# Modulation steps ahead of the scan's item, each fold with its own PSUM pair, in a one-core diffusion step

## The chip, the cores and the metric

The kernel runs on one core of a Trainium2 chip. The metric is the device time of one execution in microseconds (us). Before the change it is 2715.37 us, the median of three runs (2713.58 to 2716.63).

## The reference

One layer of a diffusion backbone works on 128 prompt tokens and 512 sample tokens, all in fp32, width 2048. Cut to what matters here:

```python
mod = silu(c) @ w_ada[l] + b_ada[l]              # 6 sections of 2048, for c and for c_ctx
sh1, sc1, g1, sh2, sc2, g2 = split(mod, 6)
h = x * (1 + sc1) + sh1
z = h @ w_in                                     # q, k, v, g, gate inputs, pooled part
log_a = log_sigmoid(a @ w_a2 + b_a) / 16         # per head, per direction
o, s = gla_chunked(q, k, v, log_a, s0)           # chunked scan, forward and backward, 4 heads
m = concat(rms_norm(o) * gain * silu(g), pool(p)) @ w_out
x = layer_norm(ALPHA * x + g1 * m)
h = x * (1 + sc2) + sh2
x = layer_norm(ALPHA * x + g2 * (silu(gate) * up) @ w_down)
```

Two of the six modulation sections, sh1 and sc1, are needed at once. The other four (sh2, sc2, g1, g2) are computed beside the projection `z = h @ w_in`, in stretches of TensorE that this document is about.

## The kernel before, in words

Every engine has its own program, written out by hand, and all of them walk one list, `SCHEDULE`. The list follows 33 units of `w_in`, each 128 output columns. A unit is four quarters (`main`) of 24 matmuls of 320 columns, since fp32 products are made of three matmuls of rounded parts (L2031 to L2033). ScalarE copies a unit's result out of PSUM (`evac`) and rounds the weights of a later unit (L977); VectorE forms their rest (L1377).

Between two quarters TensorE may leave the projection for an excursion. An excursion holds one item of the scan of a head `h` and a direction `d`, and until the modulation is done two ada steps, here called the pair of steps. The items are

- `gate`: the gate's matmul (L2072, from L2112); then VectorE takes a minimum (L1529), ScalarE the absolute value (L1129), exponential and logarithm, and VectorE the cumulative sum,
- `vT`: five transposes of v (L2103), which ScalarE copies out (L1122),
- `score`: five transposes (L2120) and then twenty records of small matmuls (L2126), with the copy L1144 and the masking L1562 behind them,
- `outer` and `outer9` (L2072, from L2144), nine outer products, which VectorE adds up to the states,
- `mix`: the output of the scan (L2161, L2166), copied or added out by VectorE (L1616 to L1619); later `norm` turns the result (L2174), after VectorE has scaled it (L1638).

An ada step multiplies 512 rows of `w_ada` (1 MB, loaded by SyncE, L689, into a ring of two slots) into four groups of 32 rows of PSUM bank 3 (L2011). After four steps ScalarE copies the bank to `high` (`adarow`, L1172). In the next excursion with a slot this row is folded: either two records of one matmul and a copy by ScalarE (`adasum`, L2191 and L1180, after which SyncE stores the row, L723), or four short matmuls and an addition by VectorE (`adacol`, L2198 and L1412). `SLOT` marks where the pair and a fold stand; `INNER` is a pair without a fold, between `outer` and `outer9`.

PSUM banks 4 and 5 are pair A, 6 and 7 are pair B. `add_pairs` gives every item its pairs in the order of the list: gate A, vT B, score B for the transposes and A for the products, outer and mix A and B, `adasum` B, `adacol` A. Before an item writes to a pair, TensorE waits in `take` until the pair's previous content has been drained.

Of the kernel before, what the change touches and what calls it, by code (L numbers as in the profile page):

```python
# [177 lines left out]
N_ADA = 16  # L178
ADA_STEPS = 4 * N_ADA
X_LOAD, X_NORM = 116, 119  # L180
SLOT, INNER = ("slot", 0, 0), ("slot", 1, 0)


def make_schedule():


    steps = []
    for n, (kind, h, j, _) in enumerate(PLAN):
        gap = [[], [], [], []]
        steps.append([n, gap])  # L190

    def put(n, quarter, *items):
        n, quarter = n + quarter // 4, quarter % 4
        steps[n][1][quarter].extend(items)

    where = {(k, h, j): n for n, (k, h, j, _) in enumerate(PLAN)}
    for h in range(HEADS):

        after_k = 4 * (where["k", h, 0] + 1)
        for at, item in ((1, ("wa", h, 0)), (2, ("state", h, 0)), (2, SLOT), (4, ("gate", h, 0)), (4, SLOT),  # L200
                         (6, ("vT", h, 0)), (6, SLOT), (6, ("cum", h, 0)), (8, ("score", h, 0)), (8, SLOT),
                         (10, ("vT", h, 1)), (10, SLOT), (12, ("outer", h, 0)), (12, INNER), (12, ("outer9", h, 0)),
                         (14, ("mix", h, 0)), (14, SLOT), (14, ("final", h, 0)),
                         (16, ("state", h, 1)), (16, ("gate", h, 1)), (16, SLOT), (18, ("cum", h, 1)),
                         (20, ("score", h, 1)), (20, SLOT),
                         (22, ("outer", h, 1)), (22, INNER), (22, ("outer9", h, 1)),
                         (24, ("mix", h, 1)), (24, SLOT), (24, ("final", h, 1)), (25, ("square", h, 0)),
                         (26, ("rms", h, 0)), (27, ("norm", h, 0)), (29, ("o_store", h, 0))):
            put(0, after_k + at, item)
    for j in range(8):  # L210
        put(where["p", j // 2, j % 2], 4, ("pool", j // 2, j % 2))
    for t in range(TT):
        if t == 0:
            put(0, X_LOAD, ("x_load", 0, 0))
        put(0, X_NORM + 2 * t, ("x_norm", t, 0))
    for g in range(4):
        put(where["p", g, 1], 7, ("poolmm", g, 0))
    flat = []
    for n, gap in steps:
        for quarter in range(4):  # L220
            flat.append(("main", n, quarter))
            if quarter == 3:
                flat.append(("evac", n, 0))
            flat.extend(gap[quarter])
    return with_modulation(flat)


def with_modulation(flat):


    out, done, behind = [], 0, []
    for item in flat:
        if item not in (SLOT, INNER):
            out.append(item)
            continue
        last = None
        if done < ADA_STEPS:
            out += [("ada", done // 4, done % 4), ("ada", done // 4, done % 4 + 1)]
            done += 2
            last = done // 4 - 1 if done % 4 == 0 else None  # L240
        if item == SLOT:
            for a in behind:
                if ADA[a // 4][1] == "col":
                    out.append(("adacol", a, 0))
                else:
                    out += [("adasum", a, 0), ("row_store", a, 0)]
            behind = []
        if last is not None:
            out.append(("adarow", last, 0))
            behind.append(last)  # L250
    assert done == ADA_STEPS and not behind
    return out


def add_pairs(flat, fills):


    used = [0, 0]
    need = {"gate": "A", "score": "AB", "outer": "AB", "outer9": "A", "mix": "AB", "norm": "AB",
            "vT": "B", "poolmm": "AB", "adasum": "B", "adacol": "A"}  # L260
    out = []
    for kind, a, b in flat:
        uses = []
        for c in need.get(kind, ""):
            x = "AB".index(c)
            uses.append((x, used[x]))
            used[x] += 1
        out.append((kind, a, b, uses))
    fills.extend(used)
    return out  # L270


FILLS = []
SCHEDULE = add_pairs(make_schedule(), FILLS)
USES = {(kind, a, b): uses for kind, a, b, uses in SCHEDULE}

# [45 lines left out]
def backbone(nc, x_all, state_gla, w_ada, w_in_b, wa2, w_pool_l, w_out, w_gu_b, w_down, consts,  # L322
# [333 lines left out]
    def _(sp):  # L656
# [144 lines left out]
        for i in range(2, N_OUT):  # L801
# [3 lines left out]
            if i == 4:  # L805
                for x in range(2):
                    sp.wait_ge(spilled[x], 16 * n_out[x])
                    sp.wait_ge(drained[x], FILLS[x])
                sp.wait_ge(row_out, 16 * 8)
# [1183 lines left out]
    def _(pe):  # L1993
# [210 lines left out]
        for x in range(2):  # L2204
            pe.wait_ge(drained[x], FILLS[x])

# [239 lines left out]
```

## Time and profile before

| | |
|---|---|
| profiled execution | 2721.88 us |
| its span | 2720.1 us |
| busy: TensorE matmul | 2643.3 us (97%) |
| busy: VectorE | 1424.9 us (52%) |
| busy: ScalarE | 898.4 us (33%) |
| busy: GpSimd | 652.8 us (24%) |
| mean granted TensorE clock | 0.991 of full speed |

TensorE is busy nearly throughout. Busy time of matmuls is modelled, since they are pipelined, so what a stretch of TensorE costs is better read from the start of one group of matmuls to the start of the next. The excursions with pairs of steps lie between about 140 and 545 us of the span; the scan of the last head, the pooling and the output projection follow.

### The profile page before, as it was taken

The page shows a single profiled execution, that of the slowest core. Times are in us where ns is not written, and L with a number is a line of the kernel's source. Part 1 is how long each engine was busy: PE and PEld are TensorE (multiplying, and loading weights), DVE is VectorE, ACT ScalarE, POOL GpSimd, SP SyncE. Part 2 cuts the span into 40 slices and gives each one's busy share as a digit, 9 for nine tenths or more (in the row PEclk, how much of TensorE's full clock was granted, in tenths as well). Part 3 has the DMA queues.
Part 4 walks back from the last instruction along what each step waited for, and adds up shares of the span by engine and source line. Part 5 has one row for each costly group of instructions (what it writes and reads, how often), then busy time and mean ns, then how long its engine had stood idle before and what let it go on. Part 6 is the DMA issues. An engine that isn't in the chain of part 4 may idle for free.

```text
span 2720.1 us, 37395 instructions
## 1 busy us (share of the span) xinstructions
PE 2643.3 (97%) x16040; PEld 2354.7 (87%) x16040; DVE 1424.9 (52%) x1680; ACT 898.4 (33%) x940; POOL 652.8 (24%) x218
## 2 busy tenths in 40 slices
PE   5999999998999999999999999999999999999997
PEld 3787877797988879999999999999999888888875
DVE  5323232346576457655555545555566354444578
ACT  4333333332311154333333333333333333333343
POOL 0000000000000001344443444344434333333440
PEclk9999999999999989999999999999999999999998
DMA  9775757422463142332233323332334645464566
GB/s 378 281 277 209 272 207 255 153 90 91 176 218 118 64 159 80 108 108 88 93 108 108 96 86 106 108 103 84 101 108 158 239 174 213 174 213 166 208 231 233
DMA packets 179384, 438.11 MB, mean 161 GB/s; under 512 B 9980, under 2 KB 25732, under 8 KB 173076
## 3 DMA queue, kind: packets, MB, share of 16 engines
q1 hardware_dynamic: 176916, 430.48, 45.4%
q10 hardware_dynamic: 2304, 5.24, 0.5%
q8 instruction: 127, 2.08, 0.3%
q14 instruction: 37, 0.30, 0.0%
HBM read 401.83 MB, written 33.85 MB: 160 GB/s over the span
## 4 chain that ended last, share of the span: by engine, by line
PE 62%; DVE 11%; DMA 10%; POOL 10%; issue 4%; ACT 3%; SPq 0%; POOLq 0%; ACTq 0%; DVEq 0%
PE ps L2355 6%; PE ps L2356 6%; PE ps L2357 6%; DMA raw_w<-w_gu_b 5%; PE ps L2278 5%; PE ps L2280 5%; PE ps L2279 5%; PE ps L2031 5%; PE ps L2033 5%; PE ps L2032 5%; POOL raw_w L945 3%; PE ps L2011 3%; DVE w_lo L1666 3%; POOL low L942 2%; POOL raw_w L948 2%
## 5 line engine op out<-in xcount | busy, mean ns | idle before, releaser
L1666 DVE TENSOR_TENSOR w_lo<-raw_w,w_hi 128x1024 fp32r<-128x1024 f32 x264 | 336.6, 1276 | 297.6 <-ACT w_hi L1210 294.7
L1210 ACT ACTIVATE w_hi<-raw_w 128x1024 fp32r<-128x1024 f32 x264 | 270.1, 1054 | 601.0 <-POOL raw_w L951 368.9
L2278 PE MATMUL ps<-x_hi,w_hi 128*128 128x320 f32 x1408 | 435.7, 309 | 1.0 <-DVE w_lo L1666 0.7
L2279 PE MATMUL ps<-x_lo,w_hi 128*128 128x320 f32 x1408 | 435.1, 309 | 0.0
L2280 PE MATMUL ps<-x_hi,w_lo 128*128 128x320 f32 x1408 | 435.1, 309 | 0.0
L942 POOL TENSOR_TENSOR low<-raw_w 128x1024 f32<-128x1024 f32 x41 | 103.7, 2528 | 1098.8 <-DMA raw_w<-w_gu_b 1058.7
L1801 DVE TENSOR_TENSOR x_lo<-low,x_hi 128x2560 fp32r<-128x2560 f32 (+2 forms) x55 | 221.3, 4027 | 262.6 <-ACT x_hi L1303 262.6
L2355 PE MATMUL ps<-w_hi,x_hi 128*128 128x512 f32 x880 | 343.8, 391 | 7.7 <-DVE w_lo L1932 2.8
L2356 PE MATMUL ps<-w_lo,x_hi 128*128 128x512 f32 x880 | 343.1, 390 | 0.0
L2357 PE MATMUL ps<-w_hi,x_lo 128*128 128x512 f32 x880 | 342.9, 390 | 0.0
L2278 PE MATMUL ps<-low_r,w_hi 128*128 128x320 f32 x1072 | 333.0, 311 | 1.5 <-DVE w_lo L1666 1.5
L2279 PE MATMUL ps<-low_r,w_hi 128*128 128x320 f32 x1072 | 332.2, 310 | 0.0
L2280 PE MATMUL ps<-low_r,w_lo 128*128 128x320 f32 x1072 | 332.1, 310 | 0.0
L2031 PE MATMUL ps<-x_hi,w_hi 128*128 128x320 f32 x1024 | 322.9, 315 | 1.8 <-DVE x_lo L1434 1.8
L2033 PE MATMUL ps<-x_hi,w_lo 128*128 128x320 f32 x1024 | 316.6, 309 | 0.0
L2032 PE MATMUL ps<-x_lo,w_hi 128*128 128x320 f32 x1024 | 316.5, 309 | 0.0
L956 POOL TENSOR_TENSOR w_lo<-raw_w,w_hi 128x2048 fp32r<-128x2048 f32 x45 | 212.5, 4723 | 352.5 <-ACT w_hi L1312 352.5
L2278 PEld LDWEIGHTS ps<-x_hi,w_hi 128*128 128x128 f32 x1408 | 264.4, 188 | 1.8 <-DVE w_lo L1666 1.3
L2279 PEld LDWEIGHTS ps<-x_lo,w_hi 128*128 128x128 f32 x1408 | 264.4, 188 | 0.0
L2280 PEld LDWEIGHTS ps<-x_hi,w_lo 128*128 128x128 f32 x1408 | 264.3, 188 | 0.0
L1377 DVE TENSOR_TENSOR w_lo<-raw_w,w_hi 128x2048 fp32r<-128x2048 f32 x48 | 110.0, 2291 | 262.8 <-ACT w_hi L977 262.7
L1312 ACT ACTIVATE w_hi<-raw_w 128x2048 fp32r<-128x2048 f32 x55 | 105.4, 1916 | 380.6 <-PE ps L2357 364.5
(238 smaller groups left out, 4362.9 us busy)
## 6 DMA issues: line engine op xcount, KB each, us to landing
raw_w<-w_gu_b SPq DMA_DIRECT2D x180, 512.0 KB, 5.6
low<-w_ada SPq DMA_DIRECT2D x68, 1024.0 KB, 6.9
raw_w<-w_down SPq DMA_DIRECT2D x55, 1024.0 KB, 5.2
low<-hidden_scratch SPq DMA_DIRECT2D x33, 1280.0 KB, 6.0
raw_w<-w_in_b SPq DMA_DIRECT2D x33, 1024.0 KB, 9.1
x_raw<-w_ada SPq DMA_DIRECT2D x25, 1024.0 KB, 15.2
raw_w<-w_out SPq DMA_DIRECT2D x16, 1024.0 KB, 5.1
hidden_scratch<-high SPq DMA_DIRECT2D x44, 320.0 KB, 5.9
```

The lines of the kernel that those rows point to most:

```text
L1210: nc.scalar.activation(weight(0, w), src, ACT.Copy).then_inc(prod_hi, 1)
L1666: nc.vector.tensor_tensor(weight(1, n), src, weight(0, n).bitcast(F32), ALU.subtract).then_inc(prod_split, 1)
L1801: nc.vector.tensor_tensor(hid_slot(x_lo, j), hid_raw(j), hid_slot(x_hi, j).bitcast(F32), ALU.subtract).then_inc(hid_split, 1)
L2031: mm(out, wh, xh, start=first, stop=False)
L2032: mm(out, wh, xl, start=False, stop=False)
L2033: ins = mm(out, wl, xh, start=False, stop=last)
L2278: mm(out, wh, version(v, 0, k), start=first and k == 0, stop=False)
L2279: mm(out, wh, version(v, 1, k), start=False, stop=False)
L2280: ins = mm(out, wl, version(v, 0, k), start=False, stop=last and k == HK - 1)
L2355: mm(ps[:, (i + 7) % 8, :], xh, rh, start=begin, stop=False)
L2356: mm(ps[:, (i + 7) % 8, :], xh, rl, start=False, stop=False)
L2357: ins = mm(ps[:, (i + 7) % 8, :], xl, rh, start=False, stop=end)
```

## The change

`SLOT` becomes `SLOT_A` and `SLOT_B`. In the list of a head's items the slot is put in front of `gate`, `vT`, `score` and `mix` instead of behind them; so an excursion now is the pair of steps, the row copy if one is due, the fold if one is due, and then the item. The excursions of `outer`, and the slot that stands by itself after `state`, stay as they are. The letter says which pair of PSUM banks the fold uses: A in front of `vT` and `score`, B in front of `gate` and `mix`.

```diff
-SLOT, INNER = ("slot", 0, 0), ("slot", 1, 0)
+SLOT_A, SLOT_B, INNER = ("slot", 0, 0), ("slot", 1, 0), ("slot", 2, 0)
...
-        for at, item in ((1, ("wa", h, 0)), (2, ("state", h, 0)), (2, SLOT), (4, ("gate", h, 0)), (4, SLOT),
-                         (6, ("vT", h, 0)), (6, SLOT), (6, ("cum", h, 0)), (8, ("score", h, 0)), (8, SLOT),
...
+        for at, item in ((1, ("wa", h, 0)), (2, ("state", h, 0)), (2, SLOT_A), (4, SLOT_B), (4, ("gate", h, 0)),
+                         (6, SLOT_A), (6, ("vT", h, 0)), (6, ("cum", h, 0)), (8, SLOT_A), (8, ("score", h, 0)),
...
-        if item == SLOT:
+        if item != INNER:
             for a in behind:
+                FOLD_PAIR[a] = item[1]
...
     need = {"gate": "A", "score": "AB", "outer": "AB", "outer9": "A", "mix": "AB", "norm": "AB",
-            "vT": "B", "poolmm": "AB", "adasum": "B", "adacol": "A"}
+            "vT": "B", "poolmm": "AB"}
...
-        for c in need.get(kind, ""):
+        for c in "AB"[FOLD_PAIR[a]] if kind in ("adasum", "adacol") else need.get(kind, ""):
```

The changed kernel has one line more above these places, so that its line numbers are higher by one. On TensorE, at the gate of head 1 in the second direction, the kernel before has the gate's two matmuls, the pair of steps and a fold of the `adacol` kind:

```order
L2033 MATMUL ps<-x_hi,w_lo 128x320
L2072 MATMUL ps<-low 128x512
L2072 MATMUL ps<-low 128x128
L2011 MATMUL ps<-low,perm 32x512 x8
L2198 MATMUL ps<-perm,high 128x2 x4
L2031 MATMUL ps<-x_hi,w_hi 128x320
```

The changed kernel has at the same place:

```order
L2034 MATMUL ps<-x_hi,w_lo 128x320
L2012 MATMUL ps<-low,perm 32x512 x8
L2199 MATMUL ps<-perm,high 128x2 x4
L2073 MATMUL ps<-low 128x512
L2073 MATMUL ps<-low 128x128
L2032 MATMUL ps<-x_hi,w_hi 128x320
```

The steps and the fold have moved ahead of the gate, and the fold is now in pair B, where the gate is in A. On ScalarE, at the first turning of v of head 1 (L1122), the kernel before copies v out and then the finished row (L1172):

```order
L1132 ACTIVATE low<-low 128x640
L1122 ACTIVATE low<-ps 128x5x128
L1172 ACTIVATE high<-ps 128x512
L1135 ACT_TABLE_LOAD
L1135 ACTIVATE perm<-perm 128x10
```

In the changed kernel the row is copied first:

```order
L1133 ACTIVATE low<-low 128x640
L1173 ACTIVATE high<-ps 128x512
L1123 ACTIVATE low<-ps 128x5x128
L1136 ACT_TABLE_LOAD
L1136 ACTIVATE perm<-perm 128x10
```

The two copies have changed places, and nothing else on ScalarE moves there. No instruction is added or removed on any engine.

## Rows read from the trace of the kernel before

**Rows 1.** Windows: span, busy time (instructions) by engine, PEclk, DMA share, GB/s.

```profile
140.00:545.00 405.00, 403.32 (x2890) 322.00 (x2889) 136.13 (x221) 133.54 (x170) 0.75 (x1) 1.00 0.63 227
545.00:665.00 120.00, 110.88 (x756) 98.48 (x755) 70.50 (x142) 38.93 (x55) 0.00 (x0) 1.00 0.24 83
```

**Rows 2.** Waits of TensorE from 140 to 545: total us, times, longest.

```profile
PE ps L2191 <- DVE low L1619: 0.9, 1, 0.9
PE ps L2198 <- ACT low L1129: 0.5, 1, 0.5
```

**Rows 3.** Timeline, all engines, a gate: start, length, engine, line, operation [idle before].

```profile
350.56 2.29 DVE L1377 TENSOR_TENSOR w_lo<-raw_w,w_hi 128x2048 fp32r<-128x2048 f32 x1 [6.62 <-ACT w_hi L977]
350.80 1.34 PE L2072 MATMUL ps<-low 33*128 33x512 f32 x4
...
352.08 1.92 PE L2011 MATMUL ps<-low,perm 128*32 128x512 f32 x16
...
352.77 0.82 DVE L1529 TENSOR_SCALAR low<-ps 128x640 f32<-128x640 f32 x1
...
353.62 0.70 ACT L1129 ACTIVATE low<-ps 128x640 f32<-128x640 f32 x1 [3.09 <-DVE low L1529]
...
354.47 1.02 PE L2198 MATMUL ps<-perm,high 128*128 128x2 f32 x8 [0.47 <-ACT low L1129]
```

**Rows 4.** Timeline of TensorE: transposes of v with a pair of steps, then without.

```profile
295.97 0.31 PE L2033 MATMUL ps<-x_hi,w_lo 128*128 128x320 f32 x1
296.12 0.71 PE L2103 MATMUL ps<-perm,low 128*128 128x128 f32 x5
296.75 1.92 PE L2011 MATMUL ps<-low,perm 128*32 128x512 f32 x16
...
298.61 0.41 PE L2031 MATMUL ps<-x_hi,w_hi 128*128 128x320 f32 x1
...
555.99 0.71 PE L2103 MATMUL ps<-perm,low 128*128 128x128 f32 x5
556.45 0.39 PE L2031 MATMUL ps<-x_hi,w_hi 128*128 128x320 f32 x1
```

**Rows 5.** Timeline of TensorE: a pair of steps by itself.

```profile
274.53 0.31 PE L2033 MATMUL ps<-x_hi,w_lo 128*128 128x320 f32 x1
274.77 1.92 PE L2011 MATMUL ps<-low,perm 128*32 128x512 f32 x16
...
276.62 0.42 PE L2031 MATMUL ps<-x_hi,w_hi 128*128 128x320 f32 x1
```

**Rows 6.** Timeline: a fold with its copy on ScalarE, then a score alone.

```profile
504.68 1.02 PE L2191 MATMUL ps<-high,perm 128*2 128x512 f32 x2
505.64 0.41 PE L2031 MATMUL ps<-x_hi,w_hi 128*128 128x320 f32 x1
...
505.74 0.59 ACT L1180 ACTIVATE high<-ps 2x512 f32<-2x512 f32 x1 [2.72 <-PE ps L2191]
...
563.86 0.71 PE L2120 MATMUL ps<-perm,low 128*128 128x128 f32 x5
564.50 0.80 PE L2126 MATMUL ps<-low 128*64 128x64 f32 x20
...
565.23 0.41 PE L2031 MATMUL ps<-x_hi,w_hi 128*128 128x320 f32 x1
```

**Rows 7.** Line L689, the 64 loads into the ring: issue to landing.

```profile
DMA to landing us min/median/max: 5.0/6.8/8.9
```

**Rows 8.** Timeline: two such loads on SyncE's queue, and the next excursion's start.

```profile
297.88 1.23 SPq L689 DMA_DIRECT2D low<-w_ada  x2
...
305.75 0.49 PE L2120 MATMUL ps<-perm,low 128*128 128x128 f32 x3
```

**Rows 9.** Timeline, head 2: VectorE's scaling, and the transposes that need it.

```profile
536.07 1.40 DVE L1638 TENSOR_SCALAR low<-low,perm 128x256 f32<-128x256 f32 x5 [2.24 <-ACT perm L1148]
...
542.87 0.38 PE L2174 MATMUL ps<-perm,low 128*128 128x128 f32 x2
```

More of the change, by code:

```diff
@@ L199, in make_schedule @@
         after_k = 4 * (where["k", h, 0] + 1)
-        for at, item in ((1, ("wa", h, 0)), (2, ("state", h, 0)), (2, SLOT), (4, ("gate", h, 0)), (4, SLOT),
-                         (6, ("vT", h, 0)), (6, SLOT), (6, ("cum", h, 0)), (8, ("score", h, 0)), (8, SLOT),
[L202 to L205, printed above, removed]
+        for at, item in ((1, ("wa", h, 0)), (2, ("state", h, 0)), (2, SLOT_A), (4, SLOT_B), (4, ("gate", h, 0)),
+                         (6, SLOT_A), (6, ("vT", h, 0)), (6, ("cum", h, 0)), (8, SLOT_A), (8, ("score", h, 0)),
+                         (10, SLOT_A), (10, ("vT", h, 1)), (12, ("outer", h, 0)), (12, INNER), (12, ("outer9", h, 0)),
+                         (14, SLOT_B), (14, ("mix", h, 0)), (14, ("final", h, 0)),
+                         (16, ("state", h, 1)), (16, SLOT_B), (16, ("gate", h, 1)), (18, ("cum", h, 1)),
+                         (20, SLOT_A), (20, ("score", h, 1)),
                          (22, ("outer", h, 1)), (22, INNER), (22, ("outer9", h, 1)),
-                         (24, ("mix", h, 1)), (24, SLOT), (24, ("final", h, 1)), (25, ("square", h, 0)),
+                         (24, SLOT_B), (24, ("mix", h, 1)), (24, ("final", h, 1)), (25, ("square", h, 0)),
                          (26, ("rms", h, 0)), (27, ("norm", h, 0)), (29, ("o_store", h, 0))):
@@ L232, in with_modulation @@
     for item in flat:
-        if item not in (SLOT, INNER):
+        if item[0] != "slot":
             out.append(item)
@@ L270, in add_pairs @@
     return out
-FILLS = []
+FILLS, FOLD_PAIR = [], {}
 SCHEDULE = add_pairs(make_schedule(), FILLS)
```

## The prediction

> **What bounds the kernel now.** I read the windows first. In the stretch that the change touches, 140 to 545 us, TensorE is busy for 403.32 of 405.00 us at a clock of 1.00, VectorE for 136.13 and ScalarE for 133.54 us [rows 1]. So TensorE sets the pace, and the other engines matter only where it waits for them. The waits of that stretch are the second view: there are two in all, 0.9 and 0.5 us [rows 2]. The third view is TensorE's timeline around an excursion, for what leaving and entering the projection costs. The last head's scan comes later, and there TensorE is busy for 110.88 of 120.00 us [rows 1]; 9.1 us are lost there, but its excursions have no pairs of steps, and the change leaves their order alone.
>
> **The waits that go.** The wait of 0.5 us is a matter of pairs. The gate of head 1 in its second direction writes pair A at 350.80. VectorE is on the weights' rest until 352.85, only then takes the minimum, and ScalarE's absolute value, which drains pair A, is done at 354.32 (353.62 + 0.70). The fold behind the steps wants pair A too and starts at 354.47, 0.47 us late [rows 3]. Ahead of the gate the fold uses pair B, and the gate is not yet in PSUM: the wait is gone. What is late next there is nothing that TensorE asks for: the gate starts 1.85 us (steps) and about 0.9 us (fold) later, VectorE is then free, and the score comes two excursions later with its own pair of steps in front, so that it is as late as the gate is. The wait of 0.9 us is a fold into pair B behind the last mix with a fold, where VectorE still adds up that mix (L1619) [rows 2]. Ahead of the mix, B was last used by the outer products, a stretch of projection earlier. Together: -1.4 us. If neither went, this term would be 0.
>
> **The moved matmuls.** There are 24 excursions in which the pair changes places with an item: 6 gates, 6 turnings of v, 6 scores, 6 mixes (one with a fold only). All instructions stay; what may change is the price of the seams. A pair by itself costs 0.24 us from the last projection matmul to its start, and 1.85 us from there to the next matmul [rows 5]. Transposes cost 0.15 us at the entry, 0.63 us up to the pair, and the pair 1.86 us: 2.64 us from 295.97 to 298.61. In the new order it is 0.24 + 1.85 + 0.46 us, the last being transposes ahead of the projection (555.99 to 556.45) [rows 4], or 2.55 us: -0.09 us each, -0.5 us for 6. A score has the same transposes first, entered for 0.15 us, then 0.64 us to its products and 0.73 us to what follows [rows 6]. In front of it the pair brings the entry of 0.24 us instead of 0.15: +0.09 us each, +0.5 us for 6. A gate is entered for the same 0.24 us as a pair, and lies 1.28 us ahead of the pair [rows 3]; I take it and the mix at 0. That is an assumption, since no row shows a pair directly ahead of a gate, a mix or transposes; the nearest rows differ by 0.09 us either way, so the bounds for 24 are -2.2 and +2.2 us. Value taken: 0.
>
> From the trace alone the sum of the seams is 0. The Trainium skill, "TensorEngine Tiling (Array Packing)", section Key Properties, speaks against this: changing the tiling mode, and not only the tile, drains TensorE. The steps use 32 columns, the score's products 64, all else here 128. Old order of a score: full, 64, 32, full, three changes; new order: 32, full, 64, full, four changes. The page has no price for one. If the excess of the pair's exit is such a price, it is 0.37 us: the pair's steps end in a gap of about 0.5 us where projection matmuls follow each other at 0.15 us. The rule would then add 6 x 0.37 = 2.2 us for the scores where I have 0.5. The row disagrees so far: leaving the 64-column products for the projection takes the score 0.73 us in all, and entering the transposes in front of them costs no more than the projection's own step [rows 6].
>
> **The folds.** A fold now stands between the steps and the item. The one new dependency on TensorE is the score's: the fold in front of it uses pair A, and the score's products use A behind their transposes. From the fold's start to the end of ScalarE's copy are 1.65 us (504.68 to 506.33), from its start to the next matmul 0.96 us, and the transposes last 0.64 us: the products would want the pair 1.60 us after the fold's start [rows 6]. With something for the signal that is 0.1 us of waiting, at two scores with this kind of fold: +0.2 us. Bounds: 0, and 0.69 us (1.65 - 0.96) at each of 16 folds if every item had to wait for the copy, 11 us. I stay near 0 because the letters A and B are dealt so that gate, turning and mix start in the other pair. On ScalarE the row's copy now stands ahead of the item's copy; it is released by the steps, which end before the item begins, so it is done or nearly done when the item is.
>
> **The ring.** The next pair of steps now starts the excursion, and its loads have less time where a long item stood before it. Take a turning of v followed by a score. Pair to pair it will be 1.85 (steps) + 0.46 (transposes) + 7.14 (projection, 298.61 to 305.75) + 0.09 (entry) = 9.54 us, and the second step starts half a pair, 0.93 us, later. The second of the two loads is issued about 0.9 us after the first (297.88), so some 2.0 us after the pair's start at 296.75 [rows 4, 8]. That leaves 8.5 us for the load. The loads take 5.0 to 8.9 us, 6.8 in the middle [rows 7]: most are in time, the slowest late by 0.4 us. I count one such wait: +0.5 us. Bounds: 0, and 0.4 us at all 24, 9.6 us. In the old order such a place had the score's 1.4 us more, less the 0.2 us that the transposes lose.
>
> **Slack elsewhere.** The transposes of `norm` have no pair of their own in front, so a mix that is later by its steps eats into their slack. For head 2 the scaling ends at 537.47 and they start at 542.87: 5.4 us of slack [rows 9], of which the change takes at most a pair and a fold, 2.8 us. Nothing. No DMA changes its place against the others on SyncE's queue by more than the items' lengths; the row's store stands where it did, behind its copy.
>
> **The sum.** -1.4 + 0 + 0.2 + 0.5 = -0.7 us, against the profiled execution of 2721.88 us (span 2720.1 us and 1.8 us around it), so 2721.2 us for such a one. The median of the runs is 6.5 us lower; what follows is TensorE-bound and passes the difference on, so I take the same -0.7 us off 2715.37: 2714.7 us. This kernel's three runs differ by 3 us, and a change below 0.2%, 5.4 us, can hardly be told from none.
>
> **Rivals.**
> 1. The seams are dearer than the sum has them: a pair followed by a 64-column or 128-column item costs more than a pair followed by the projection. For: every exit from the steps shows the gap. Against: the gap belongs to the steps, of which there are as many. With 2.2 us instead of 0 for the seams: +1.5 us, 2716.9 us. This is also where the skill's rule on draining ends up.
> 2. Nothing changes: one of the two waits comes back at another fold, at the same price. 2715.4 us.
> 3. Slower: the ring runs dry. Every moved pair starts earlier within its round, and the loads share the DMA engines with the loads of the projection's weights. If the second load lands after 8.9 us as a rule and not as an exception, 24 x 0.4 = 9.6 us come on top of -1.2: +8.4 us, 2723.8 us. It decides from a mean lateness of 0.28 us over the 24 pairs (6.6 us), a landing time of 8.8 us on average against 6.8 now. For: two slots only. Against: in this stretch no step waits for a load now.
> 4. Faster beyond the waits: with its modulation work done earlier in each excursion VectorE enters the last head's scan ahead, and some of the 9.1 us lost there [rows 1] are saved. If two thirds are, -6.1 - 0.7 = -6.8 us, 2708.6 us. Against: these waits are inside one head's scan, and each starts from a matmul of that head.
>
> **How the numbers follow.** The forecast has 0.62, rival 1 0.12, rival 2 0.09, rival 3 0.08, rival 4 0.09. The first three lie within 0.2% (2709.9 to 2720.8): same 0.83, faster 0.09, slower 0.08. The unknown terms of the forecast span about 2 us to either side, and the median of a few runs another 1.5; with a part of rivals 3 and 4 the range is 2710 to 2719.5 us.
>
> **What would show it.** In the changed profile: no wait of a fold for L1130 or L1620 between 140 and 545 us (else the first term is wrong); from the last projection matmul to the next, 2.55 us for transposes with a pair (else the seams); a score's products starting within 0.2 us after their transposes when a fold stands in front (else the folds); and waits of the steps for `w_ada` below 1 us in all (else the ring). Forecast and rival 2 differ by less than the runs do, so only these rows tell them apart. A time outside 0.2% would prove the account of the stretch wrong.

## The result, and the profile after

| | before | after |
|---|---|---|
| median of 6 runs | 2716.38 us (2713.58 to 2718.88) | 2724.94 us (2720.0 to 2728.58) |
| ratio, 95% interval | | 1.0024 [1.0014, 1.0034] |
| profiled execution, span | 2721.88, 2720.1 us | 2728.58, 2726.8 us |
| mean granted TensorE clock | 0.991 | 0.989 |

The change made the kernel slower by 0.24%, where -0.03% was forecast. The ratio is an estimate of its own and not the quotient of the medians: by it the difference is 6.5 us, while the medians are 8.6 us apart. 12 more runs of the changed kernel gave 1.003 [1.002, 1.004], with medians 7.0 us apart. The windows of [rows 1] read after the change (columns as there):

```profile
140.00:545.00 405.00, 402.37 (x2854) 318.69 (x2853) 135.53 (x216) 131.34 (x166) 0.75 (x1) 1.00 0.64 230
545.00:665.00 120.00, 114.43 (x774) 102.51 (x773) 65.56 (x126) 36.87 (x51) 0.00 (x0) 0.99 0.23 80
```

In the same 405 us the trace has 2854 matmuls of TensorE, 2890 before. The waits of TensorE in this stretch (total us, times, longest) have one row:

```profile
PE ps L2032 <- ACT low L1078: 2.1, 2, 1.1
```

Both rows of [rows 2] are gone, as forecast. In their place the projection itself (L2032) waits for ScalarE's copy of q (L1078). This wait has no counterpart before, and it belongs to no pair of banks.

What the totals can't show is where the time went, since the engines' work is the same. I cut the trace at the first projection matmul of every unit and compare the lengths. Units 3 to 21 (the excursions with pairs of steps) take 410.63 us before and 415.40 after; units 22 to 31 are equal to 0.05 us wherever the clock is the same. (It isn't in unit 27, which holds 3.4 to 10.3 us at half the clock in every trace, and at varying places in units 24 to 26.) A stretch of 3.4 us at half the clock costs 1.5 us and lies in unit 13 in this trace of after; by the second profile of the same kernel (e7 below), whose stretch lies elsewhere (in unit 10), the difference without such stretches can be read unit by unit:

| units | before | after | sum of differences |
|---|---|---|---|
| 8, 14, 20 | 22.89, 22.00, 22.89 | 24.45, 23.46, 24.45 | +4.58 |
| 5, 11, 17 | 20.84, 20.89, 20.84 | 21.15, 21.30, 21.23 | +1.11 |
| 13, 21 | 18.80, 22.98 | 18.39, 22.04 | -1.35 |
| the other eleven | | | +0.23 |

The sum is +4.57 us. (The two profiled spans differ by 6.7 us: 3.2 us arise in the prologue ahead of unit 3, which isn't changed, 4.8 in these units, -1.3 behind them, stretches at half the clock among all three.) Units 13 and 21 held the two waits of [rows 2]; units 8, 14 and 20 are where the second direction of a head ends and the next head's q is copied out. Below is the timeline of all engines there (start, length, engine, line, operation [idle before and what ended it]), before:

```profile
218.70 1.34 PE L2072 MATMUL ps<-low 33*128 33x512 f32 x4
...
220.66 0.82 DVE L1529 TENSOR_SCALAR low<-ps 128x640 f32<-128x640 f32 x1
...
229.07 0.83 DVE L1545 TENSOR_TENSOR low<-perm,low 128x640 f32<-128x640 f32 x1
...
232.43 0.83 DVE L1553 TENSOR_TENSOR low<-low 128x640 f32<-128x640 f32 x1
...
233.37 0.77 ACT L1077 ACTIVATE low<-ps 128x320 f32<-128x320 f32 x2 [0.97 <-DVE low L1553]
...
234.25 0.36 PE L2031 MATMUL ps<-x_hi,w_hi 128*128 128x320 f32 x1
```

and after:

```profile
222.20 1.92 PE L2012 MATMUL ps<-low,perm 128*32 128x512 f32 x16
224.05 1.34 PE L2073 MATMUL ps<-low 33*128 33x512 f32 x4
225.43 0.82 DVE L1530 TENSOR_SCALAR low<-ps 128x640 f32<-128x640 f32 x1 [1.18 <-PE ps L2073]
226.29 0.70 ACT L1130 ACTIVATE low<-ps 128x640 f32<-128x640 f32 x1 [1.51 <-DVE low L1530]
...
233.84 0.83 DVE L1546 TENSOR_TENSOR low<-perm,low 128x640 f32<-128x640 f32 x1
...
237.20 0.82 DVE L1554 TENSOR_TENSOR low<-low 128x640 f32<-128x640 f32 x1
238.14 0.77 ACT L1078 ACTIVATE low<-ps 128x320 f32<-128x320 f32 x2 [0.97 <-DVE low L1554]
238.96 0.41 PE L2032 MATMUL ps<-x_hi,w_hi 128*128 128x320 f32 x1 [1.05 <-ACT low L1078]
```

To be seen: from the gate to the end of q's copy a chain runs through VectorE and ScalarE, 15.44 us before (218.70 to 234.14) and 14.86 after (224.05 to 238.91). The copy overwrites q of the previous head, so in `evac` it waits for the last product with q (`qe_done`), and also for the last product with k (`ke_done`, set at L1554), which doesn't read q. The copy in turn frees a bank that the projection needs: main banks rotate over three (`main_bank`), two for each unit, so the second half of a unit's first quarter goes to the bank where the first half of the unit before still lies. Before, the copy ended at 234.14 and that matmul came at 234.25: 0.1 us spare. After, the gate stands behind its pair of steps and is 1.85 us late against the projection (from gate to the unit's start 13.79 us before, 11.93 after), VectorE is freer at that moment (1.38 us from the gate to the minimum, L1530, and 1.96 us before, L1529), and TensorE waits 1.05 us at this place. The sum comes out: 1.86 us late, less 0.58 us by which the chain is shorter, less 0.1 us that were spare, is 1.2 us; the matmul comes 1.76 us after its unit's start before (232.49) and 2.98 us after it now (235.98), 1.2 us later.

In the first direction the same bank limit is met by v. Its copy was issued 0.80 us after unit 11's start (302.23) before and 1.15 us after it (307.43) now, here before and after:

```profile
303.03 0.75 ACT L1084 ACTIVATE low<-ps 128x320 f32<-128x320 f32 x2
```

```profile
308.58 0.74 ACT L1085 ACTIVATE low<-ps 128x320 f32<-128x320 f32 x2
```

It ends at 309.32, and the matmul that takes the bank starts at 309.38, 0.34 us after the matmul ahead of it instead of 0.15. Before, the copy ended at 303.78 and that matmul came at 303.99: 0.2 us spare. This is 0.2 us of what units 5, 11 and 17 lose; the rest is the seam of the score in them.

The seams, of [rows 4] and [rows 6], in after. TensorE's timeline at a turning of v with its pair, then at a score with a pair and a short fold:

```profile
301.21 0.31 PE L2034 MATMUL ps<-x_hi,w_lo 128*128 128x320 f32 x1
301.45 1.92 PE L2012 MATMUL ps<-low,perm 128*32 128x512 f32 x16
303.31 0.77 PE L2104 MATMUL ps<-perm,low 128*128 128x128 f32 x5
303.83 0.39 PE L2032 MATMUL ps<-x_hi,w_hi 128*128 128x320 f32 x1
```

```profile
311.33 1.92 PE L2012 MATMUL ps<-low,perm 128*32 128x512 f32 x16
313.18 1.05 PE L2199 MATMUL ps<-perm,high 128*128 128x2 f32 x8
314.10 0.74 PE L2121 MATMUL ps<-perm,low 128*128 128x128 f32 x5
314.77 0.80 PE L2127 MATMUL ps<-low 128*64 128x64 f32 x20
315.50 0.42 PE L2032 MATMUL ps<-x_hi,w_hi 128*128 128x320 f32 x1
```

The turning takes 0.24 + 1.86 + 0.52 = 2.62 us, where 2.55 was worked out and 2.64 was there before. The score's transposes and products cost 0.67 and 0.73 us, against 0.64 and 0.73 before; with its own entry a score adds 0.14 us, and 0.15 more at two of the six, where a row's fold stands ahead (e6 below: 0.30 us at units 8 and 20, 0.15 at 5 and 14). The steps' exit in front of transposes is no dearer than in front of the projection: in both cases 0.52 us pass from the last matmul of the steps to the next one.

### The profile page after: what moved, and what is told of

It is laid out like the page before. It is cut to its first block, busy times and chain, and to the rows that moved or that the text cites. A ratio compares the mean times of both kernels' runs of the same rounds, so it can differ in the third digit from the quotient of the medians.

```text
span 2726.8 us, 37396 instructions
## 1 busy us (share of the span) xinstructions
PE 2650.2 (97%) x16040; PEld 2359.8 (87%) x16040; DVE 1429.7 (52%) x1680; ACT 898.4 (33%) x940; POOL 651.2 (24%) x218
## 4 chain that ended last, share of the span: by engine, by line
PE 79%; DVE 8%; DMA 5%; POOL 3%; ACT 3%; issue 2%; SPq 0%; POOLq 0%; ACTq 0%; DVEq 0%
PE ps L2279 10%; PE ps L2280 10%; PE ps L2281 10%; PE ps L2356 6%; PE ps L2357 6%; PE ps L2358 6%; PE ps L2032 5%; PE ps L2034 5%; PE ps L2033 5%; PE ps L2012 3%; PE ps L2226 3%; PE ps L2227 2%; PE ps L2228 2%; PE ps L2073 2%; DMA raw_w<-w_gu_b 2%
## 5 line engine op out<-in xcount | busy, mean ns | idle before, releaser
L2032 PE MATMUL ps<-x_hi,w_hi 128*128 128x320 f32 x1024 | 325.8, 318 | 4.0 <-ACT low L1078 2.1
```

The lines of the kernel that those rows point to most:

```text
L2032: mm(out, wh, xh, start=first, stop=False)
```

## The experiments

All kernels below start from the changed one, in which the pair and the fold have a letter; their lines are 4 or 5 higher than those of the kernel before. A kernel's ratio is against the kernel before on the same chip (35 runs in each of three batches, medians 2719.13, 2718.13 and 2718.43 us). Single runs of one kernel differ by up to 12.5 us, mostly with the granted clock, so I judge by the lengths of units, which repeat to 0.03 us in two traces of one kernel where the clock is the same, and take the ratio beside them.

| kernel | ratio | unit 8 | unit 14 | unit 20 | units 3 to 21 |
|---|---|---|---|---|---|
| before again (e8) | 1.0002 [0.9993, 1.001] | 22.90 | 22.01 | 22.89 | 410.64 |
| after again (e7) | 1.003 [1.002, 1.004] | 24.45 | 23.46 | 24.45 | 416.72* |
| folds only (e1) | 1.0012 [1.0003, 1.0022] | 22.88 | 22.00 | 22.88 | 409.14 |
| folds only again (e9) | 0.9999 [0.9991, 1.0008] | 22.89 | 22.00 | 22.90 | 409.18 |
| second gate behind no pair (e2) | 1.0012 [1.0004, 1.0021] | 23.17 | 22.16 | 23.17 | 412.74* |
| q's copy waits for less (e3) | 1.0013 [1.0004, 1.0023] | 23.37 | 22.15 | 23.36 | 415.18** |
| only that gate behind a pair (e4) | 1.0013 [1.0004, 1.0022] | 24.16 | 23.32 | 24.16 | 413.12 |
| only v behind a pair (e5) | 1.0002 [0.9993, 1.0011] | 22.88 | 22.00 | 22.88 | 409.67 |
| only scores behind a pair (e6) | 1.0007 [0.9999, 1.0016] | 23.19 | 22.16 | 23.19 | 411.88 |
| only first gate behind a pair (e10) | 0.9997 [0.9988, 1.0005] | 22.88 | 22.00 | 22.88 | 410.78* |
| first gate behind no pair (e13) | 1.0013 [1.0004, 1.0022] | 24.45 | 23.47 | 24.45 | 415.08 |
| fold ahead of its pair (e14) | 1.0009 [1.0, 1.0018] | 24.28 | 23.47 | 24.29 | 413.39 |

Each * is a stretch of 3.4 us at half the clock, 1.5 us, in that total.

**e7, the changed kernel once more**, with nothing edited, to see whether the slowdown stands.

> The changed kernel once more, to be timed beside the next three. Bank theory: in the second direction's gate (3 times) the chain gate, scan, q*exp, k*exp, copy of the next head's q out of PSUM ends 1.05 us too late for the projection's banks, 1.4 us with the refill; turnings of v cost 0.3 us each at 3 places; scores 0.14 us each, short folds 0.07 us each, against 1.5 us of waits that went: 4.9 us above the kernel before. Seam theory: the same 4.9 us, but spread over all 24 moved pairs at 0.2 us each. Clock theory: the matmuls cost the same, and the two kernels met different half-speed stretches by chance; then this one is within 1.5 us of the kernel before.

Measured: 2726.14 us, 1.003 [1.002, 1.004]. The slowdown is there, and the wait shows at all three heads (the row of the waits of TensorE, 140 to 560 us; L2036 is the projection's first matmul, L1082 the copy of q):

```profile
PE ps L2036 <- ACT low L1082: 3.1, 3, 1.1
```

In the first trace of after the third place, unit 14, didn't wait, because a stretch at half the clock from 361.2 us had made TensorE late itself.

**e1, the folds' letters alone**, in the old order of items and slots. A fold behind a gate or a score uses pair B, behind a turning or a mix pair A:

```diff
-(4, SLOT_B), (4, ("gate", h, 0)), (6, SLOT_A), (6, ("vT", h, 0)),
+(4, ("gate", h, 0)), (4, SLOT_B), (6, ("vT", h, 0)), (6, SLOT_A),
-(8, SLOT_A), (8, ("score", h, 0)),
+(8, ("score", h, 0)), (8, SLOT_B),
...
-(14, SLOT_B), (14, ("mix", h, 0)),
+(14, ("mix", h, 0)), (14, SLOT_A),
-(16, SLOT_B), (16, ("gate", h, 1)),
+(16, ("gate", h, 1)), (16, SLOT_B),
...
```

> The order of the kernel before, the pair of steps behind every item, but each fold in the PSUM pair that its excursion's item leaves first: B behind gates and scores, A behind turnings and mixes. All theories: the 0.5 us wait of the fold behind a gate goes, the 0.9 us wait behind the last mix goes down to some 0.1 us. Bank and seam theory: 1.3 us below the kernel before, 6 below the changed one. Clock theory: no difference to either that repeats.

Measured: the waits of 140 to 560 us are all gone, and units 3 to 21 are 1.49 us shorter than before. The first term of the prediction (-1.4 us) is this part of the change, and it needs only the letters. The ratio of 1.0012 [1.0003, 1.0022] doesn't agree with a shorter scan; e9 repeated it.

**e2, the second direction's gate back in front of its pair**, all else as in after:

```diff
-(16, SLOT_B), (16, ("gate", h, 1)),
+(16, ("gate", h, 1)), (16, SLOT_B),
```

> The changed kernel with the pair behind the gate again in the second direction only (3 of the 24 moved pairs), the fold still in B. Bank theory: no wait of the projection for the copy of q; 4.2 us less than the changed kernel, so 0.7 us above the kernel before. Seam theory: 3 of 24 seams undone, 0.6 us less than the changed kernel. Clock theory: no difference.

Measured: no wait of TensorE from 140 to 560 us; unit 8 is 23.17 us, 1.28 less than in after. So the three waits come from this one move. The gate's chain starts at 220.38, 13.79 us ahead of unit 8 as in the kernel before, and q's copy is through in time.

**e3, q's copy waits only for the product that it overwrites**, all else as in after:

```diff
-                    act.wait_ge(qe_done, 2 * h)
-                    act.wait_ge(ke_done, 2 * h)
+                    act.wait_ge(qe_done if kind == "q" else ke_done, 2 * h)
```

> The changed kernel in its order, but ScalarE's copy of q out of PSUM waits only for the product that reads the old q (qe_done) and no longer for the one that reads the old k (ke_done), which costs about 0.95 us of the chain. Bank theory: the wait of the projection for L1078, 1.05 us, goes down to 0.1 us, 3 to 4 us less than the changed kernel in all, 1 to 2 above the kernel before. Seam and clock theory: as the changed kernel, 4.9 us or nothing above the kernel before.

Measured (timeline of ScalarE, VectorE and the weight load of TensorE, at the place shown above; L1555 and L1557 are the two products with k, the second sets `ke_done`; the product with q, L1553, was done at 234.14):

```profile
234.06 0.82 DVE L1555 TENSOR_TENSOR low<-low 128x640 f32<-128x640 f32 x1
...
234.82 0.74 ACT L1081 ACTIVATE low<-ps 128x320 f32<-128x320 f32 x2
234.95 0.83 DVE L1557 TENSOR_TENSOR low<-low 128x640 f32<-128x640 f32 x1
...
235.62 0.19 PEld L2035 LDWEIGHTS ps<-x_hi,w_hi 128*128 128x128 f32 x1 [0.22 <-ACT low L1081]
```

The copy starts before the last product with k, and the projection's wait shrinks to 0.22 us. The gate is as late as in after; only the length of the chain behind it is cut, and the units of 24.45 us fall to 23.37. Together with e2 this shows the path from gate over copy to bank: cut at the gate's end the wait goes, cut at the copy's end it nearly goes. e3 has a loss of its own in unit 17, 21.69 us where the changed kernel has 21.23: there a step waits for the ring (0.2 us of it is in the view of waits).

**e8, the kernel before once more.**

> The kernel before, timed against itself. If the comparison has no bias of its own, the ratio is 1 within its interval (about 0.1%, 2.7 us) and the mean granted clock is that of the kernel before, 0.9917 in 35 runs. If whatever stands in the tested place is slower by 3 us and at 0.990, the excess of the folds-only kernel was a bias.

Measured: 1.0002 [0.9993, 1.001], the two waits of [rows 2] at 0.9 and 0.5 us again. This is what the comparison gives for no change.

**e9, the edit of e1 once more.**

> The folds-only kernel a second time; its TensorE needed 1.4 us less in the scan, yet its runs were 0.12% above the kernel before, with a mean clock of 0.9901. Chance theory: now within 0.1% of the kernel before or below it, its clock 0.9915. Clock theory (something in it draws more half-speed stretches): again 0.1% above, at 0.990.

Measured: 0.9999 [0.9991, 1.0008]; units 3 to 21 take 409.18 us. The scan is 1.45 to 1.49 us shorter in the two traces, and the two ratios differ by 0.13%, more than twice the gain that is looked for (0.05%). The 1.0012 of e1 did not repeat; whether the kernel as a whole gains 1.4 us can't be told by these runs.

**e4, only the second direction's gate behind its pair**, the rest as in e1:

```diff
-(16, ("gate", h, 1)), (16, SLOT_B),
+(16, SLOT_B), (16, ("gate", h, 1)),
```

> The folds-only kernel with the pair in front of the gate in the second direction alone (3 of 24). Bank theory: the projection's wait for L1078 is back with 1.05 us or a little less, units 8, 14 and 20 take 24.2 us instead of 22.9 and 23.3 instead of 22.0; 4 us above the folds-only kernel. Seam theory: 0.2 us for each of the three, 0.6 us above it.

Measured: units 8, 14 and 20 are 1.28, 1.32 and 1.28 us longer than in e1, units 3 to 21 together 3.98, and no other part of the change is in this kernel. The row of its waits:

```profile
PE ps L2036 <- ACT low L1082: 3.2, 3, 1.1
```

The ratio is 1.0013 [1.0004, 1.0022].

**e6, only the scores behind their pairs**, the rest as in e1:

```diff
-(8, ("score", h, 0)), (8, SLOT_B),
+(8, SLOT_A), (8, ("score", h, 0)),
```

and the same at quarter 20.

> The folds-only kernel with the pair in front of the score alone (6 of 24). The score's seam costs 0.14 us at each, and the two or three folds with a copy by ScalarE another 0.15 us: 1.2 us above the folds-only kernel in the scan, no wait for L1078; a larger difference in time would be the clock's. Seam theory with 0.2 us each: the same 1.2 us.

Measured: units 3 to 21 take 2.74 us more than e1's, where 1.2 was expected. 1.2 us of it is the ring in unit 11, where the pair takes 3.07 us to the next group instead of 1.85; the second step waits for its load:

```profile
PE ps L2016 <- DMA low<-w_ada: 1.0, 1, 1.0
```

Another 0.3 us goes the same way in unit 17, too short a wait for that view: the second step's load lands 4.74 us into the unit, the step starts at 4.78, and the pair takes 2.17 us instead of 1.85. The rest is the score's seam, 0.15 us at each of the six and 0.15 more at units 8 and 20. In after itself no step waits for the ring from 140 to 560 us, since there the neighbouring pairs have moved too; in e3 it was the one in unit 17.

**e5, only the turnings of v behind their pairs**, the rest as in e1:

```diff
-(6, ("vT", h, 0)), (6, SLOT_A),
+(6, SLOT_A), (6, ("vT", h, 0)),
```

and the same at quarter 10.

> The folds-only kernel with the pair in front of the turnings of v alone (6 of 24). Bank theory: with the first turning of each head the copy of v (L1085 in the changed kernel) comes some 0.1 us too late for the bank; units 5, 11 and 17 take 0.2 to 0.3 us more in this step, nothing at the second turning; 0.7 us above the folds-only kernel in the scan.

Measured: +0.5 us for units 3 to 21; units 5, 11 and 17 are 0.17, 0.25 and 0.25 us longer. This is v's copy and its bank. The time is 1.0002 [0.9993, 1.0011].

**e10 and e13, the first direction's gate.** e10 puts only it behind its pair, e13 takes only it back in front, from after:

```diff
# e10, from e1
-(4, ("gate", h, 0)), (4, SLOT_B),
+(4, SLOT_B), (4, ("gate", h, 0)),
# e13, from after
-(4, SLOT_B), (4, ("gate", h, 0)),
+(4, ("gate", h, 0)), (4, SLOT_B),
```

> The folds-only kernel with the pair in front of the gate in the first direction alone (3 of 24; one of them, in unit 10, has a short fold). No wait for L1078 in any theory, and the same time as the folds-only kernel in the scan to 0.2 us. Clock theory: in more than half of the executions a half-speed stretch in unit 10, which then takes 22.5 us instead of 21.0; 1 us in the median. Without it: unit 10 takes 21.0 us.

> The changed kernel with the pair behind the gate again in the first direction alone. Bank theory: the waits for L1078 stay, units 8 and 20 take 24.5 us; 0 to 0.3 us less than the changed kernel. Clock theory: no half-speed stretch in unit 10, 1 us less in the median.

Measured: in e10 units 3 to 21 are 1.6 us longer than e1's, all of it in unit 10. The windows before, in and after a stretch of it (columns as in [rows 1]):

```profile
286.00:290.60 4.60, 4.60 (x33) 2.71 (x26) 0.94 (x3) 0.00 (x0) 0.00 (x0) 1.00 0.60 182
290.60:294.00 3.40, 3.40 (x15) 3.40 (x14) 0.12 (x1) 3.19 (x4) 0.00 (x0) 0.50 1.00 305
294.00:303.00 9.00, 9.00 (x67) 7.39 (x66) 3.36 (x5) 2.86 (x4) 0.00 (x0) 1.00 0.71 262
```

PEclk is 0.50, 1.2 GHz, for 3.4 us, right behind this excursion (TensorE's timeline):

```profile
285.68 1.92 PE L2016 MATMUL ps<-low,perm 128*32 128x512 f32 x16
287.53 1.05 PE L2203 MATMUL ps<-perm,high 128*128 128x2 f32 x8
288.51 1.34 PE L2077 MATMUL ps<-low 33*128 33x512 f32 x4
289.79 0.41 PE L2036 MATMUL ps<-x_hi,w_hi 128*128 128x320 f32 x1
```

The time as a whole is 0.9997 [0.9988, 1.0005] all the same. In this trace a half-speed stretch that lies near 976 us in before, e1 and e9 (10 to 14 us long) is absent; what the clock did in the other eleven runs was not profiled. e13 has no stretch at unit 10, keeps the waits at units 8, 14 and 20, and comes to 1.0013 [1.0004, 1.0022] with 415.08 us for units 3 to 21. So the first gate's place isn't what makes after slow. (e13's ratio is 0.0017 below that of e7, more than its scan explains; more on that below.)

**e14, the fold ahead of its pair**, in `with_modulation`, from after: the short fold and the gate are no longer neighbours.

```diff
-        if done < ADA_STEPS:
-            out += [("ada", done // 4, done % 4), ("ada", done // 4, done % 4 + 1)]
...
         if item != INNER:
             for a in behind:
...
+        if done < ADA_STEPS:
+            out += [("ada", done // 4, done % 4), ("ada", done // 4, done % 4 + 1)]
...
```

> The changed kernel with the fold ahead of the pair of steps, so that fold, steps and item follow each other and the steps part the fold from the gate. Bank theory alone: the wait for L1078 stays, 1.05 us three times; the scan as in the changed kernel less 0.3 us. Clock theory added (a short fold directly ahead of a gate, 2.25 us of narrow matmuls in a row, is what the clock falls after in units 10 and 13, in 5 of 8 places so far, at 1.56 us each): no half-speed stretch in units 10 and 13, and 2 us less than the changed kernel in the median, so 5 to 6 above the kernel before instead of 7 to 8.

Measured: units 3 to 21 are 1.8 us shorter than in e7, leaving half-speed stretches aside, where 0.3 was expected. There is no half-speed stretch in them, and the clock stays at 1.00 where e10 has 0.50, with TensorE's timeline and the windows

```profile
287.60 0.95 PE L2203 MATMUL ps<-perm,high 128*128 128x2 f32 x8
288.48 1.92 PE L2016 MATMUL ps<-low,perm 128*32 128x512 f32 x16
290.33 1.34 PE L2077 MATMUL ps<-low 33*128 33x512 f32 x4
```

```profile
286.00:290.60 4.60, 4.60 (x38) 3.15 (x37) 2.25 (x2) 1.12 (x2) 0.00 (x0) 1.00 0.01 3
290.60:294.00 3.40, 3.40 (x20) 2.79 (x20) 0.82 (x1) 1.40 (x2) 0.00 (x0) 1.00 0.98 316
```

The DMA engines are idle here in the first window where e10 has them at 0.60, so the order isn't the only difference between the two. (DMA doesn't tell the places of the changed order apart either: from 3.0 us ahead of the gate to 1.4 us behind its start the share is 0.42 to 0.47 at all ten of them, with a stretch and without.) The three waits for q's copy stay (3.2 us in all). The ratio is 1.0009 [1.0, 1.0018], 0.0021 or 5.7 us below that of e7, which ran in another batch; units 3 to 21 account for 1.8 us of that. The rest is open: it is of the size by which two sets of runs of one kernel differ (e1 and e9). Against e13, in the same batch, e14 is 2.4 us faster by the medians (2720.93 and 2723.28), and the scan gives 1.7.

## Why the prediction was wrong

**The step that failed** is the one that let the gate be late: "What is late next there is nothing that TensorE asks for". I followed the gate's chain only as far as the score, which comes with a pair in front of it and is as late as the gate is. (In the second direction, the gate that is discussed there, the score is the very next excursion, not two later; it has a pair in front all the same.) A second consumer hangs on the chain: the next head's q can be copied out only when the previous head's products are done, and that copy frees a bank of the projection, which has no pair in front and is not later. It had 0.1 us to spare (234.14 against 234.25). The later gate cost 1.3 us at each of three heads (e4: 1.28, 1.32, 1.28 at units 8, 14 and 20); e2 takes it away again, and e3 most of it (1.1 of 1.3 us at unit 8 and at unit 20). That there was only 0.1 us to spare couldn't be seen in the waits, since nothing waited.

**The waits that go**: right in mechanism and size. Both rows of [rows 2] are gone, and units 13 and 21 are 1.35 us shorter together (-1.4 forecast). e1 shows that the letters do this without the move.

**The moved matmuls**: near. 0.52 us instead of 0.46 for transposes behind steps, so a turning saves 0.02 us and not 0.09. A score costs 0.14 us more and not 0.09, six times. Gates and mixes, taken at 0, cost 0 to 0.09 us: units 6, 7, 18 and 19 are as long as before, units 9, 12 and 15 (a short fold in front of a mix) and 13 (one in front of a gate, against e1) 0.08 to 0.09 us longer. The bounds of 2.2 us to either side hold. The Trainium skill ("TensorEngine Tiling (Array Packing)", Key Properties) says that a change of tiling mode drains TensorE, and gives no price. The prediction's estimate of one, 0.37 us, isn't borne out in that size: a score has one change more now and costs 0.14 us more, and the 64-column products are left within 0.73 us as before.

**The folds**: right in mechanism; the score stalls 0.15 us behind a row's fold, where 0.1 was forecast.

**The ring**: 0.5 us was counted, no wait was there in after. It isn't far off: with only the scores moved (e6) it costs 1.5 us at two places.

**Slack elsewhere** was read only at `norm`, where it was right. v's copy had about as thin a slack as q's (0.2 us) and wasn't looked at; by e5 it costs 0.17 to 0.25 us at each of units 5, 11 and 17, 0.67 us.

**The rivals.** 1, dearer seams: not in that size. 2, a wait comes back at another fold: no. 3, the ring: no, though its time (2723.8) is close to the measured one; a right time for a wrong reason. 4, a faster end: units 22 to 26, most of the last head's scan, are the same to 0.05 us at the same clock. The sign was that of rival 3, the mechanism none of mine.

**The size.** The scan accounts for +4.57 us: q's copy +3.9, v's +0.7, the scores' seams and stalls +1.1 to 1.2, the two waits -1.35, and some 0.2 spread over the rest. The measured difference is +6.5 us (interval 3.8 to 9.2), in the second set +8.2 (5.4 to 10.9). So the scan covers the lower part of it; the last 2 to 4 us are not pinned down. They need not belong to the change: of the four kernels timed in e7's batch each is 1.7 to 3.9 us further above the kernel before, by the medians, than its scan is (leaving half-speed stretches aside), e1 too, in which nothing is moved. Compared with each other they fit: e7 is 4.6 us above e1 by the medians, and 6.1 by the scan. In the other two batches this excess is -0.6 to 1.8 us, and e13, with nearly the whole loss in its scan (+4.5 us), comes to +4.9 us by the medians. The mean clock was 0.9902 in e7's runs against 0.9917 of the runs of before beside them, and within the runs of one kernel 0.001 of clock goes with about 1.3 us, which would be 2 us. Why the clock should be lower is not shown. The places told of in the last section are a candidate, but e10, which has one, isn't slower, and e1, which has none, has as low a mean clock (0.9901).

The best version is the letters without the move (e1, e9): 1.45 us shorter in the scan than before, not to be told from it in time.

## What to carry to other kernels

Before an operation is moved later behind other work of the same engine, follow its whole chain to every consumer on the pacing engine, those through buffer releases too, and write down the time between the release and the instruction that needs it: a view of waits shows only the slack that is negative, and 0.1 us of slack looks just like 5. Where a change has two parts, here the dealing of pairs and the order, try the part that removes the wait alone. When runs of one kernel spread more than the effect, the lengths of fixed stretches of the program (here units of the projection, same to 0.03 us) tell what the total can't.

## What the runs showed of the hardware

After pair, short fold and gate directly in a row, TensorE's clock fell to half (1.2 GHz) for 3.4 us at 6 of 10 such places in units 10 and 13 of all profiles (unit 10: e7, e2, e3, e10, not after; unit 13: after, e3, not e7, e4, e13), and at none of the 18 places with another order. Each costs 1.5 us. What TensorE did in the 2.3 us before the projection resumed are matmuls of 2 columns and of 33 rows, with the steps of 32 columns ahead of them. In e14 the same instructions with the fold ahead of the steps left the clock at 1.00. It is a tendency, not a rule: the same kernel had it at unit 10 in one execution and not in another.

Half-speed stretches of 3.4 us or multiples also fall at varying places in all kernels, the kernel before among them, and go with about half of the spread of single runs (2712.46 to 2724.97 us for it on one chip): in the three batches of 35 runs the mean clock accounts for 40 to 52% of the variance of the time.
